# MLP down projection: pairs of output blocks as seven products of sums (Strassen) instead of eight, in the first three of four quarters

## The reference, cut to what matters

```python
def sq_relu_mlp(h, w_up, w_down):
    return jnp.square(jax.nn.relu(h @ w_up)) @ w_down
```

## Time and profile before

| | |
|---|---|
| three runs, median (lowest to highest) | 1431.69 us (1431.62 to 1432.69) |
| profiled execution, span | 1430.9 us |
| TensorE matmuls | 1387.0 us busy, 97%, 11481 of them |
| VectorE | 687.7 us, 48% |
| ScalarE | 490.8 us, 34% |
| GpSimd | 321.2 us, 22% |
| mean granted TensorE clock | 0.990 |

### The profile page before, as it was taken

One profiled execution on the slowest core, in us unless ns is written; L12 is line 12 of the kernel. 1 busy time (PEld: TensorE's weight loads), 2 busy tenths in 40 slices (PEclk: granted clock), 3 DMA queues, 4 the chain that ended last, 5 costly groups with the idle time before them and its releaser, 6 DMA issues.

```text
span 1430.9 us, 28766 instructions
## 1 busy us (share of the span) xinstructions
PE 1387.0 (97%) x11481; PEld 1274.8 (89%) x11481; DVE 687.7 (48%) x1174; ACT 490.8 (34%) x939; POOL 321.2 (22%) x284
## 2 busy tenths in 40 slices
PE   7999997999999999999999999999999999999997
PEld 7656665698999999999988888899999999999996
DVE  4457785437433334434366544544653343333435
ACT  5356662326312212212254433343541221221222
POOL 2220024020703404205410000001151250330531
PEclk9999998999999999999999999999999999999999
DMA  9400023231323232232314133222233323333321
GB/s 253 122 9 1 1 67 105 66 99 45 109 84 88 88 88 84 78 88 88 92 45 143 53 107 107 86 93 79 59 104 89 88 88 88 88 88 88 89 60 63
DMA packets 203904, 120.32 MB, mean 84 GB/s; under 512 B 13990, under 2 KB 199616, under 8 KB 203808
## 3 DMA queue, kind: packets, MB, share of 16 engines
q1 hardware_dynamic: 197776, 104.74, 25.4%
q0 software_dynamic: 6032, 14.24, 3.1%
HBM read 111.37 MB, written 7.59 MB: 83 GB/s over the span
## 4 chain that ended last, share of the span: by engine, by line
PE 88%; DVE 8%; ACT 2%; issue 2%; DMA 0%; DVEq 0%; SPq 0%; ACTq 0%
PE ps L1969 64%; PE ps L2031 7%; PE ps L2360 2%; PE ps L2196 1%; DVE y L1404 1%; PE ps L2177 1%; DVE ps L1562 1%; PE ps L2378 1%; PE ps L2291 1%; PE ps L2229 1%; DVE x L1414 1%; PE ps L1993 1%; PE ps L2532 1%; PE ps L2530 1%; DVE act_lo L1420 1%
## 5 line engine op out<-in xcount | busy, mean ns | idle before, releaser
L878 ACT CAST w_hi<-w_raw 128x1024 fp32r<-128x1024 f32 x172 | 180.3, 1050 | 670.3 <-PE ps L1969 642.1
L1969 PE MATMUL ps<-act_hi,w_hi 128*128 128x280 f32 (+1 forms) x1408 | 297.3, 292 | 1.8 <-DVE act_lo L1666 0.9
L1969 PE MATMUL ps<-act_hi,w_lo 128*128 128x280 f32 (+1 forms) x1408 | 295.1, 291 | 0.0
L1969 PE MATMUL ps<-act_lo,w_hi 128*128 128x280 f32 (+1 forms) x1408 | 294.0, 290 | 0.0
L1370 DVE TENSOR_TENSOR w_lo<-w_raw,w_hi 128x1024 fp32r<-128x1024 f32 x172 | 252.7, 1471 | 57.5 <-ACT w_hi L878 57.3
L1969 PEld LDWEIGHTS ps<-act_hi,w_hi 128*128 128x128 f32 x1408 | 223.0, 189 | 8.0 <-issue 6.8
L1969 PEld LDWEIGHTS ps<-act_hi,w_lo 128*128 128x128 f32 x1408 | 223.7, 189 | 0.0
L1969 PEld LDWEIGHTS ps<-act_lo,w_hi 128*128 128x128 f32 x1408 | 222.6, 189 | 0.0
L1969 PE MATMUL ps<-h_hi,w_lo 128*128 128x280 f32 (+1 forms) x928 | 193.8, 290 | 0.0
L777 POOL TENSOR_TENSOR relu<-relu 128x560 f32<-128x560 f32 (+1 forms) x64 | 85.5, 1336 | 481.3 <-DVE relu L1689 417.8
L1969 PE MATMUL ps<-h_hi,w_hi 128*128 128x280 f32 (+1 forms) x928 | 193.1, 289 | 0.0
(11 more groups left out here) (332 smaller groups left out, 1844.5 us busy)
## 6 DMA issues: line engine op xcount, KB each, us to landing
w_raw<-in_mlp_w_up_dram SPq DMA_DIRECT2D x64, 512.0 KB, 4.0
w_raw<-in_mlp_w_down_dram SPq DMA_DIRECT2D x64, 512.0 KB, 3.6
w_raw<-in_gla_w_in_dram SPq DMA_DIRECT2D x24, 512.0 KB, 3.8
pg_ckv<-in_cache_ckv_dram SPq DMA_DIRECT2D x64, 128.0 KB, 2.3
w_raw<-in_mla_w_o_dram SPq DMA_DIRECT2D x8, 512.0 KB, 4.7
sts<-in_state_gla_dram POOLq DMA_DIRECT2D x4, 1024.0 KB, 6.4
out_dram<-sts POOLq DMA_DIRECT2D x4, 1024.0 KB, 5.1
w_raw<-in_gla_w_o_dram SPq DMA_DIRECT2D x8, 512.0 KB, 3.6
```

The source lines that it names most:

```text
L878: nc.scalar.copy(w_hi[slot(g)][:], w_raw[raw_slot(g)][:]).then_inc(w_rounded, 1)
L1969: last = nc.tensor.matmul(out[:, h, 0:n], w[:, c, :], a[:, c, t0 + n * h:t0 + n * h + n], start=(c == 0 and k == 0), stop=(c == DC - 1 and ...
```

## The change

In each of the first three quarters of both layers (`CROSSED = 3`) the 8 down blocks become 4 pairs. A pair is a product of 2 x 2 parts: two output blocks by two halves of the tokens, with the chunks of even and of odd number as the two inner parts. It is worked out in Winograd's form of Strassen's scheme, with seven products of 12 matmuls each (4 chunk pairs, three matmuls each, one half of the tokens), 84 matmuls in place of 96. The fourth quarter and all up blocks keep their matmuls.

- Sums of weights for each pair: GpSimd makes S1, S2, S3 from the two loaded blocks (`weight_forms`), VectorE makes S4 in place in `w_raw[1]` (`fourth_form`), 512 elements a partition each. A pair now has four groups of weights (the first block; S2 and S1; the second block with S4; S3, half as large) and each is rounded and split, in place of two.
- Sums of hidden activations: VectorE makes four forms of 280 columns for each two up blocks (T1 in `first_form`, the others in `other_forms`), ScalarE rounds them (`form_high`), VectorE subtracts (`first_low`, `other_low`). They come while the up blocks run.
- Outputs: seven reads of PSUM by VectorE for a pair in place of two evictions.
- `h_hi` and `h_lo` have seven units of 4 x 280 columns each in place of 8 x 560 columns. GpSimd's square has two buffers `h2` of its own.
- The order is written out for a whole quarter, and the semaphores count 24 weight groups and 36 products a quarter. Six semaphores that are raised once became one (`once_mm`).

The core of the diff (`Q_GROUPS = 24`, `Q_ITEMS = 36`; `CROSS_LAST = (3, 5, 6, 7)` is the product of a pair after which each of its four weight buffers is free). The functions are, in this order, of SyncE, GpSimd, ScalarE, VectorE (three) and TensorE:

```diff
+            def load_pairs(layer, q):
+                g0 = G_MLP[layer]
+                for i in range(Q_PAIRS):
+                    for s in range(RAW):
+                        sp.wait_ge(w_split, q * Q_GROUPS + (g0 + (cross_group(i - 1, 2) if i else 6 + s) + 1))
+                        sp.dma_start(w_raw[s][:], cols(mlp_w_down[layer][bass.ds(q * D, D), :], (2 * i + s) * P))\
+                            .then_inc(w_loaded[s], 16)
...
+            def weight_forms(layer, q, i):
+                raw, raw2 = w_raw
...
+                pool.wait_ge(w_loaded[0], q * 128 + pair_raws(layer, i))
+                pool.wait_ge(w_loaded[1], q * 128 + pair_raws(layer, i))
...
+                nc.gpsimd.tensor_tensor(s1, raw2[:, 0:DC:2, :], raw2[:, 1:DC:2, :], ALU.add).then_inc(s_made, 1)
+                pool.wait_ge(s_made, k + 1)
+                nc.gpsimd.tensor_tensor(s2, s1, raw[:, 0:DC:2, :], ALU.subtract).then_inc(s_made, 1)
+                if i:
+                    pool.wait_ge(w_split, q * Q_GROUPS + (G_MLP[layer] + cross_group(i - 1, 3) + 1))
+                nc.gpsimd.tensor_tensor(s3_form[:], raw[:, 0:DC:2, :], raw2[:, 0:DC:2, :], ALU.subtract).then_inc(s_made, 1)
+            def crossed_quarter(layer, q, first):
+                for k in range(8):
+                    hidden_low(layer, q, k, relu[2] if first and k == 2 else relu[k % 2], True)
+                    if k == 4:
+                        weight_forms(layer, q, 0)
+                for i in range(1, Q_PAIRS):
+                    weight_forms(layer, q, i)
...
+            def round_pair(layer, q, i, s):
...
+                slot_free(layer, q, at)
...
+                elif s == 1:
+                    act.wait_ge(s_made, q * 12 + (made + 2))
...
+                elif s == 2:
+                    act.wait_ge(w_loaded[1], q * 128 + pair_raws(layer, i))
+                    act.wait_ge(s4_made, q * 4 + (layer * CROSSED * 4 + i + 1))
...
+            def fourth_form(layer, q, i):
+                dve.wait_ge(s_made, q * 12 + (layer * CROSSED * 12 + 3 * i + 3))
...
+            def up_step(layer, q, k):
+                if k < SPLIT:
+                    split_up(layer, q, k + SPLIT)
+                else:
+                    split_pair(layer, q, 0, k - SPLIT)
+                if k % 2 == 0:
+                    if k:
+                        other_low(layer, q, k // 2 - 1)
+                    first_form(layer, q, k // 2)
+                else:
+                    first_low(layer, q, k // 2)
+                    other_forms(layer, q, k // 2)
+                if k == 5:
+                    fourth_form(layer, q, 0)
...
+                read(1, y[:, j, first], a, fresh=True)
+                if i == 0:
+                    other_low(layer, q, 3)
+                read(2, y[:, j:j + 2, second], both(b), fresh=True)
+                read(3, y[:, j, first], c, before=1)
+                following(0)
+                read(4, y[:, j, second], d, before=2)
+                read(5, y[:, j, second], a, before=4)
+                if i < Q_PAIRS - 1:
+                    fourth_form(layer, q, i + 1)
+                following(1)
+                read(6, y[:, j + 1, first], d, fresh=True)
+                following(2)
+                read(7, halves(y[:, j + 1, t0:T]), both(a), before=6)
+                following(3)
...
+            def pair_products(layer, q, i):
...
+                weights_ready(1)
+                if i == 0:
+                    read(0)
+                for p in range(4):
+                    forms_ready(2 * p)
+                    last = chunk_product(b, 1, p, T1, p)
...
+                read(1)
+                for p in range(4):
+                    forms_ready(2 * p + 1)
+                    last = chunk_product(a, 1, 4 + p, T2, p, start=False)
+                last.then_inc(blk_mm, 1)
+                read(4)
+                for p in range(4):
+                    last = chunk_product(d, 2, 2 * p + 1, T4, p)
+                last.then_inc(blk_mm, 1)
+                weights_ready(3)
+                read(5)
```

More of the change, by code:

```diff
@@ new lines, in crossed_quarter @@
+            def crossed_quarter(layer, q, first):
+                for k in range(8):
+                    if k < SPLIT:
+                        round_up(layer, q, k + SPLIT)
+                    else:
+                        round_pair(layer, q, 0, k - SPLIT)
+                    hidden_high(layer, q, k, relu[2] if first and k == 2 else relu[k % 2], True)
+                    form_high(layer, q, k)
+                for i in range(1, Q_PAIRS):
+                    for s in range(4):
+                        round_pair(layer, q, i, s)
+                for k in range(SPLIT):
+                    round_up(layer, q + 1, k)
@@ L1209, in _ @@
+            def mlp(layer):
+                crossed_quarter(layer, 0, True)
+                with act.Fori(1, CROSSED) as q:
+                    crossed_quarter(layer, q, False)
+                for k in range(8):
+                    round_block(G_MLP[layer] + CROSSED * Q_GROUPS + k + SPLIT)
+                    hidden_high(layer, CROSSED, k, relu[k % 2], False)
             mlp(0)
@@ L2033, in half_chunk, with hidden_chunk, last_chunk @@
                 return last
+            def hidden_chunk(out, g, c, h):
+                n = out.shape[-1]
+                for k, (w, a) in enumerate(((w_hi, h_hi), (w_hi, h_lo), (w_lo, h_hi))):
+                    last = nc.tensor.matmul(out, w[slot(g)][:, c, :], a[:, token_half(c, h), c // 2, 0:n], start=(c == 0 and k == 0),
+                                            stop=(c == DC - 1 and k == 2))
+                return last
             def last_blocks(u, ins):
+                def last_chunk(out, g, c, h):
+                    return hidden_chunk(out, g, c, h) if u % 2 else half_chunk(out, g, c, ins, part(u, h))
                 g = G_LAST[u]
@@ new lines, in down_block @@
+            def down_block(layer, u, j):
+                g = G_LAST[u] + j
+                pe.wait_ge(w_split, g + 1)
+                pe.wait_ge(blk_read, read_at(g) - 1)
+                out = blk_ps(g)
+                for c in range(DC):
+                    if j == 0:
+                        pe.wait_ge(h_ready, layer * 32 + CROSSED * 8 + c + 1 + 2)
+                    for k, (w, a) in enumerate(((w_hi, h_hi), (w_hi, h_lo), (w_lo, h_hi))):
+                        for h in range(2):
+                            last = nc.tensor.matmul(out[:, h, :], w[slot(g)][:, c, :], a[:, token_half(c, h), c // 2, 0:out.shape[-1]],
+                                                    start=(c == 0 and k == 0), stop=(c == DC - 1 and k == 2))
+                last.then_inc(blk_mm, 1)
```

495 lines of the change are left out of this document (340 added, 155 removed).

## The result

The changed kernel takes **1478.38 us** (median of four runs, 1475.82 to 1482.78) against 1431.65 us of the kernel before in runs on the same chip. The ratio is 1.033, 95% interval 1.031 to 1.034. It is slower by 46.7 us, where the forecast had 33. The profile is of the slowest of the four executions (1482.78 us), so its span is 50.1 us longer than that of the earlier trace rows.

The account below looks back on a forecast made before the run. It took TensorE's matmuls as the bound, with VectorE and GpSimd taking turns. A down stage of 16.8 + 10.8 + 2 x 13.6 = 54.9 us against 49.4, six times, adds 33 to 1430.9; 0.8 more gives 1464.7 us, range 1442 to 1492.

Parts of the forecast that it names:

- What bounds the kernel; the saving: TensorE's matmuls bound the kernel; 0.1286 us a matmul, 1.54 us saved a pair, 37 us over 24 pairs without waits.
- The turns of VectorE and GpSimd: While one works on two SBUF inputs the other stands; a VectorE split then takes 2.11 us, not 1.23.
- Pair 0: First pair of a down stage: waits of 1.97, 1.31, 0.53 and 2.15 us at products 2, 5, 5 and 6; 16.8 us.
- Pair 1: Second pair of a down stage: its weights became ready during the first pair, so it takes 10.8 us, without waits.
- The ring: Pairs 2 and 3: chain from loads through forms, S4, splits and a read to the next loads; 13.6 us once round.
- Six equal quarters: Each changed down stage takes 54.9 us against 49.4, +5.5; six such quarters give +33 us, in both layers.
- the up stage stays TensorE's: Up stages: VectorE's and GpSimd's mutually exclusive parts are 5.1 us of a 6.17 us block, so no waits; 49.4 us.
- Waits of "some 70 us": TensorE's new idle time that the profile would show, some 70 us, released by VectorE.
- The prediction's own signs of being wrong: Pairs at 10.8 us, waits in up stages, new products' matmuls over 0.129 us apart, or a chain part off by over 1 us.
- The forms keep up: Rival: pairs take 10.8 us, pair 0 some 11 to 12; about 1398 us; needs chain below 12.35, pair 0 below 13; chance 0.12.
- No turns: Rival: VectorE and GpSimd work side by side; pair 0 11.3 us, pairs 2 and 3 13.4; 1429 us; chance 0.05.
- Worse still: Rival: each GpSimd form takes 1.93 us on top of the turns; chain 15.6 us, pair 0 20.6; 1511 us; chance 0.07.

Follow-up runs that it names:

- e2: The changed kernel, but ScalarE makes the float32 squares that GpSimd made; 1457.04 us, ratio 1.016 to the kernel before.
- e8: The changed kernel, but GpSimd's forms of pair 1 wait until VectorE has made T4 of pair 0; 1473.58 us, ratio 1.030 to the kernel before.
- e1: The changed kernel, but SyncE loads a pair's first block once S4 of the pair before is made; 1455.04 us, ratio 1.0155 to the kernel before.
- e7: The changed kernel with one more GpSimd subtraction of 512 elements ahead of S3 in pairs 2 and 3; 1497.14 us, ratio 1.045 to the kernel before.
- e9: The changed kernel, but VectorE reads products 4 and 5 ahead of the split of the next pair's first block; 1469.34 us, ratio 1.026.
- e3: The changed kernel with the edits of e1 and e2 together; 1425.91 us, ratio 0.9945 to the kernel before.
- e6: The changed kernel with the edits of e1 and e2, and ScalarE rounding hidden forms one step later; 1412.07 us, ratio 0.985 to the kernel before.
- e4: The changed kernel with 14 useless matmuls ahead of TensorE's wait at product 6 of pairs 0, 2 and 3; 1480.93 us, ratio 1.033.

## Why the prediction was right in sign and short in size

- **What bounds the kernel; the saving.** Right. In the up stages of the later quarters TensorE is full, and matmuls at full clock start 0.128 us apart in the new products too. Some 36 us were saved, 37 forecast.
- **The turns of VectorE and GpSimd.** Right, by e2 and e8: 0.43 us against 1.55 for the same instruction.
- **Pair 0, 16.8 us.** 17.4 and 17.3 in layer 0, 15.7 and 14.8 in layer 1 (later quarters). The waits at product 2 (1.97 forecast, 1.92) and product 6 (2.15; 1.85) came as laid out, product 5's last quarter waited 0.2 instead of 0.53, and the 1.31 at product 5 was missing. The prediction let GpSimd's first form run ahead of VectorE's T2; but the second block of pair 1 landed at 503.84, 4.8 us behind the start of pair 0, when T2 was already running (503.66), so VectorE waited one turn less. In e1, where the form does come first, that wait is there (1.12). What filled the gap is the half clock, 2.1 us: 10.8 + 4.45 + 2.1 = 17.4. So the two errors nearly cancel, and that 16.8 came so close is luck. Each of the prediction's four waits also holds 0.10 us that it does not name (4.57 - 2.70 is 1.87 and not 1.97); TensorE did start 0.05 to 0.10 us behind VectorE's end.
- **Pair 1, 10.8 us.** 10.8 in the second quarter alone; in the other five stages it waits at product 6 and takes 11.3 to 11.9.
- **The ring, 13.6 us.** 13.9 in layer 0. e7 lengthens it and is paid in full, e1 shortens it and the waits go, e9 shows that the wait at product 6 is the ring's. Between pairs 2 and 3 of the second quarter the second block lands 5.9 us behind the first one's issue (5.4 forecast), GpSimd's start and three forms take 4.5 (4.5), S4 0.7 (0.8), the two splits and the read 2.6 (2.65), SyncE 0.2 (0.25). So what was short is the loads, by 0.5 us. TensorE's waits of 0.4 and 2.2 us there had been put at 0.9 and 2.0.
- **Six equal quarters: the step that failed most.** "Six such quarters: +33 us" and "the up stage stays TensorE's" hold roughly for the four later ones (56.1, 55.8, 55.0, 53.9 us; forecast 54.9 in layer 0, and 5.5 us above the 48.1 of before in layer 1). The two first ones took 57.9 and 57.2. By the profiled spans the sum is 17.1 us short (50.1 against 33.0): 6.6 us of it are the first quarters' down stages, 5.0 the up stages ahead of them, 3.8 the four later down stages, 1.7 the rest of the kernel. In the first quarters ScalarE rounds hidden forms ahead of the next weights, VectorE waits for ScalarE, and GpSimd's squares push VectorE further: up block 5 waits 1.3 to 1.4 us, and products 1 and 2 wait 1.5 and 1.3 for a `h_lo` and for the eviction of up block 7. The prediction said that both engines would be late when the last up block ends, but priced it from one steady stage and took no stage with a backlog. It also put GpSimd at 2.2 us a block, where the shortest square and subtraction of the earlier trace rows add up to 2.51, so that the parts that exclude each other are some 5.4 us of 6.17 and not 5.1. e3 against e6 puts 6 us on it in each first quarter once the ring is short; in the changed kernel itself it is about 2.5 us of up stage and 2 to 3 us of down stage a layer.
- **The clock: the term that was not in the sum.** 17.3 us of matmuls at the 1.2 GHz level in the six stages, 12.8 of them behind the waits of pair 0. The trace before has granted clock 1.00 in both stages and the prediction priced a matmul by it throughout. Across all runs slowness goes with the waits (2.1 us with 14.5 of waits, 26.4 with 70.9), and it stands only behind waits; but which wait brings it is open, as e4 and e7 show. In pair 2 a slow stretch only fills what would be a wait of pair 3 (15.5 + 12.4 us in e8 against 13.9 + 14.0); in pair 3 it is paid (13.9 + 15.4 in e2).
- **Waits of "some 70 us".** 62.3 in these stages.
- **The prediction's own signs of being wrong.** Two of them came: waits in the up stages (1.3 and 1.4 us at up block 5 of the first quarters) and matmuls farther apart than 0.129 us. TensorE's busy time, forecast to fall by 37 us, fell by 7.
- **Rivals.** "The forms keep up" did not come in this kernel, and its condition was the right one: e6, with a ring of 12.2 us between pairs 2 and 3 (under 12.35) and pair 0 at 11.9 to 12.3 (under 13), is faster than the kernel before, though 14 us above the rival's price of 1398. "No turns" is refuted by e8. "Worse still" did not come: in the ring only the first form meets VectorE (1.7 to 1.9 us), the other two take 1.31.

By size: 43.4 us in the down stages are 62.3 + 17.3 - 36; the forecast had 70 - 37 = 33, with more waits and no clock. What stays open is what brings the clock down behind some waits, how much the kernel would gain at full clock with its waits unchanged, and why product 6 of pair 0 waits less in layer 1, where the pair is 1.6 to 2.5 us shorter.
